# Leaving out three filling products per layer in the router's chain of an encoder kernel

## The reference

```python
g_prob = softmax(xf @ w_group + b_group)            # 4 groups
g_w, g_sel = top_k(g_prob, 1)
e_logits = (xf @ w_router + b_router) of the 8 experts in the picked group
top_v, top_i = top_k(e_logits, 2)
weights = g_w * softmax(top_v)
y = for each token and picked expert e: (silu(x @ w1[e]) * (x @ w3[e])) @ w2[e]
h = h + sum over the two picks of weights * y
```

## Time and profile before

| | before |
|---|---|
| median of three runs | 1776.87 us |
| lowest and highest | 1775.58, 1777.07 us |
| profiled execution, device time | 1775.46 us |
| its span, first to last instruction | 1773.7 us |
| PE busy | 1504.0 us, 85% |
| VectorE busy | 617.1 us, 35% |
| ScalarE busy | 528.3 us, 30% |
| mean granted clock of PE | 0.938 |
| read from HBM | 524.63 MB |

### The profile page before, as it was taken

How to read it: one execution, slowest core, us unless ns; L and a number is a source line. 1 busy time by engine, 2 the same in 40 slices (tenths; PEclk the granted TensorE clock), 3 DMA queues, 4 the chain that set the end, 5 groups by cost and what they waited for, 6 DMA issues and landing times.

```text
span 1773.7 us, 24555 instructions
## 1 busy us (share of the span) xinstructions
PE 1504.0 (85%) x9704; PEld 1009.0 (57%) x9704; DVE 617.1 (35%) x1020; ACT 528.3 (30%) x829; POOL 57.3 (3%) x100
## 2 busy tenths in 40 slices
PE   8999999999886867676799999999998767676766
PEld 7788889896332323232277878998863233333322
DVE  5565777644110000000054668775530101010101
ACT  6434655553200000000163465635431000000001
POOL 3021000000000000000000200000000000000000
PEclk9999999999988888889899999999999988898989
DMA  7545235755999999999955453357469999999997
GB/s 230 190 141 191 102 138 190 274 201 198 405 423 422 422 421 423 422 422 421 416 184 176 125 182 115 136 198 285 150 277 408 422 422 421 422 423 421 422 423 309
DMA packets 118166, 530.92 MB, mean 299 GB/s; under 512 B 8809, under 2 KB 9001, under 8 KB 68935
## 3 DMA queue, kind: packets, MB, share of 16 engines
q1 hardware_dynamic: 114944, 524.13, 74.3%
q0 software_dynamic: 3136, 5.73, 1.6%
q10 hardware_dynamic: 12, 0.05, 0.0%
HBM read 524.63 MB, written 1.05 MB: 296 GB/s over the span
## 4 chain that ended last, share of the span: by engine, by line
PE 55%; DMA 36%; DVE 3%; SPq 2%; ACT 2%; issue 2%; PEldq 0%; POOL 0%; DVEq 0%; ACTq 0%
DMA ring<-in_w_dram 35%; PE ps L2031 11%; PE ps L1667 7%; PE ps L1672 6%; PE ps L1668 6%; PE ps L1701 5%; PE ps L1702 5%; PE ps L1707 5%; SPq L557 2%; PE ps L1749 2%; PE ps L1806 1%; PE ps L2000 1%; PE ps L1829 1%; PE ps L1760 1%; PE ps L1618 1%
## 5 line engine op out<-in xcount | busy, mean ns | idle before, releaser
L2031 PE MATMUL ps<-ring,big 128*32 128x512 f32 x2048 | 299.0, 738 | 205.8 <-DMA ring<-in_w_dram 204.0
L1129 DVE TENSOR_TENSOR weight_split<-ring,weight_split 128x1024 fp32r<-128x1024 f32 x224 | 270.9, 1222 | 168.4 <-ACT weight_split L730 165.7
L2031 PEld LDWEIGHTS ps<-ring,big 128*32 128x32 f32 x2048 | 83.3, 131 | 416.1 <-issue 415.9
L730 ACT ACTIVATE weight_split<-ring 128x1024 fp32r<-128x1024 f32 x224 | 234.3, 1058 | 223.5 <-PE ps L1707 93.0
L1528 DVE TENSOR_TENSOR big<-big,ps 128x256 f32<-128x256 f32 x32 | 13.5, 421 | 696.8 <-ACT big L1018 696.8
L1667 PE MATMUL ps<-operand_split,weight_split 128*128 128x256 f32 x896 | 228.6, 293 | 5.0 <-DVE operand_split L1194 4.4
L1668 PE MATMUL ps<-operand_split,weight_split 128*128 128x256 f32 x896 | 220.5, 283 | 0.0
L1667 PEld LDWEIGHTS ps<-operand_split,weight_split 128*128 128x128 f32 x896 | 171.7, 192 | 18.9 <-issue 17.3
L1014 ACT ACTIVATE big<-ps 128x512 f32<-128x512 f32 x32 | 33.6, 1050 | 474.5 <-PE ps L2031 474.5
L1668 PEld LDWEIGHTS ps<-operand_split,weight_split 128*128 128x128 f32 x896 | 172.1, 192 | 2.0 <-issue 1.9
L1701 PE MATMUL ps<-weight_split,operand_split 128*128 128x512 f32 x384 | 152.8, 398 | 5.2 <-issue 5.2
(11 more groups left out here) (243 smaller groups left out, 1359.8 us busy)
## 6 DMA issues: line engine op xcount, KB each, us to landing
ring<-in_w_dram SPq DMA_DIRECT2D x376, 1024.0 KB, 17.8
ring<-in_w_in_dram SPq DMA_DIRECT2D x28, 2048.0 KB, 8.1
ring<-in_w_xkv_dram SPq DMA_DIRECT2D x8, 2048.0 KB, 8.1
ring<-in_w_attn_out_dram SPq DMA_DIRECT2D x4, 2048.0 KB, 8.3
ring<-in_w_conv_out_dram SPq DMA_DIRECT2D x4, 2048.0 KB, 7.7
ring<-in_w_out_dram SPq DMA_DIRECT2D x4, 2048.0 KB, 8.1
big<-in_w_dram SPq DMA_DIRECT2D x8, 1024.0 KB, 13.7
ring<-in_w_xq_dram SPq DMA_DIRECT2D x4, 2048.0 KB, 8.6
```

The lines of the kernel that those rows point to most:

```text
L730: act.activation(split_quarter(k, 0), landed_quarter(k), ACT.Copy).then_inc(w_hi, 1)
L1129: dve.tensor_tensor(split_quarter(k, 1), landed_quarter(k), split_quarter(k, 0).bitcast(F32), ALU.subtract).then_inc(w_lo, 1)
L2031: last = pe.matmul(ps[CAP * j:CAP * (j + 1), 1, :], xe[:, k, e * CAP:(e + 1) * CAP], pair_slot(j)[:, k, :], start=(k == 0), stop=(k == DC ...
```

## The change

PE no longer issues the three filling products per layer; the helper `again` goes with them. Nothing else changes: the order of the other instructions, the waits, and the other engines are as they were. The banks into which the three wrote are written again by others, before they are read, as before.

```diff
-                def again(count, idle):
-
-                    for _ in range(count):
-                        pe.matmul(ps[:, idle, :], ident, h[:, 1, 0:SLAB], start=True, stop=True)
-
-                again(2, bank("nf3"))
                 pe.wait_ge(*due(r_mask, 1))
                 dst = ps[:, bank("rank"), :]
                 pe.matmul(dst[:, 0:EXPERTS], tri, picked[:, 0, :], start=True, stop=True)
...
-                again(1, bank("router1"))
                 pe.wait_ge(*due(n_ready_act, 4))
                 first_tokens()
                 pair(first=True)
```

## The result

| | before | changed |
|---|---|---|
| median, 22 executions each | 1777.12 us | 1783.97 us |
| lowest and highest | 1773.78, 1782.13 | 1773.75, 1788.22 |
| ratio, 95% interval | | 1.0029 [1.0019, 1.0039] |
| profiled execution, device time | 1775.46 | 1787.15 |
| its span | 1773.7 | 1785.4 |

The change makes the kernel slower, by 0.29% as a ratio and 6.9 us between the medians. The forecast was 1783.5. Single executions spread more than the difference is large, and those of the changed kernel fall into two groups with nothing between: seven from 1773.75 to 1778.54 and fifteen from 1782.26 to 1788.22.

What follows compares the result with a forecast made beforehand. PE's router chain at the expert stage's door was taken to bound the end, the DMA engines waiting there. The profiled 1775.46 us plus 5.5 (layer 0) and 2.6 (layer 1) gave 1783.56, say 1783.5; range 1778.0 to 1785.5.

Steps and rivals of the forecast that it cites:

- The door bounds the end: From the last router products to the first expert pair, DMA waits for PE: a microsecond there is one at the end.
- Layer 0 gets no time back: Layer 0's rank products wait for VectorE's picked experts anyway, so removing the fillings gives back 0 us.
- early fall: Low clock around L1949 and L1974, before the rank products; seen in layer 1, 1298.0 to 1304.7 us; may shift or stay.
- Layer 1 gets 1.5 us back: Layer 1's rank products queue behind the fillings; without them they start 1.72 us earlier, of which 1.5 us is saved.
- The clock falls late: Idle and sparse PE work around the rank products drops the clock to 0.50 at about the gather's start.
- Price of the gather, 3.1 us: The gather's 32 instructions at the low clock take 0.2125 instead of 0.115 us each: 3.1 us, bounds 0 and 3.8.
- Price of the first pair, 2.3 us: The first expert pair's L2031 begins at the low clock and loses 1.7 to 3.35 us, taken as 2.3.
- The sum: Late fall's price at layer 0's door 5.5 us, bounds 1.7 and 7.2; layer 1 adds 2.6 net.
- B: Rival: the clock falls late in one layer only, the other gets its 1.5 us: 1779.5 us, chance 0.26.
- C: Rival: the clock stays high at both doors and PE merely gets out of the way: 1773.9 or 1772.9 us, chance 0.08.
- D: Rival: the clock falls but returns during the gather; a 3.4 us low stretch costs 1.7 once: 1777.2 us, chance 0.07.
- E: Rival: the DMA-bound experts absorb the door's delay: 1775.5 us, or 1774.0 with layer 1's gain, chance 0.05.

Runs made afterwards that it cites:

- e3: Ten filling products instead of two ahead of the rank products, against the kernel before: median 1791.07 us, ratio 1.0080.
- e8: The change itself run once more, all three fillings out in both layers, against the kernel before: median 1783.82 us, ratio 1.0039.
- e10: The three fillings left out in layer 1 only, against the kernel before: median 1778.91 us, ratio 1.0011.
- e7: Residual product moved before the last transposes, half-wide filling before the router's products; of the old fillings only the last kept; against the kernel before: 1790.57 us, ratio 1.0079.
- e6: Residual product moved before the last transposes, half-wide filling before the router's products; none of the three old fillings; against the kernel before: 1787.68 us, ratio 1.0062.
- e2: Only the filling behind the rank products left out, the two ahead kept, against the kernel before: median 1785.76 us, ratio 1.0049.
- e1: The two fillings ahead of the rank products left out, the one behind kept, against the kernel before: median 1777.45 us, ratio 1.0002.
- e11: Residual product and half-wide filling moved into early gaps, fillings ahead of the rank products kept, last one left out; against the kernel before: 1785.26 us, ratio 1.0045.

## Why the prediction held, step by step

- **The door bounds the end.** Right. Shown by e3: two doors 13.0 us longer than in the profile of before, a median 14.1 higher.
- **Layer 0 gets no time back.** Right: with no early fall the rank products wait for VectorE whether PE fills or not. With an early fall, which layer 0 did not have in the profile I worked from, it can get time back as layer 1 does (e8, 22.89 us).
- **Layer 1 gets 1.5 us back.** The mechanism is right where the early fall lasts long: 1.3 us in e10. In the changed kernel's own profile the early stretch of layer 1 lasted 3.2 us instead of 6.7; PE was 0.68 us idle before the picks came, and about 0.9 us was saved. That is an estimate: in e3's layer 1, with an early stretch of the same length, the first filling starts 7.05 us behind L1949's start, two fillings are 1.72, and the rank products of the changed kernel start at 7.90. They start 2.5 us sooner than in layer 1 of before, mostly because the early fall was shorter.
- **The clock falls late.** Right, in both layers of the changed profile, but not at the gather's start: it came some 2 us into the gather (started at 432.22 and 1313.24; low from 434.4 and 1315.0).
- **Price of the gather, 3.1 us.** Right for a whole gather at the low clock (e7: 3.1, e6: 3.3). The late fall of the changed profile came only 2 us into it: +1.5 and +1.9. In e8 it was +2.8.
- **Price of the first pair, 2.3 us.** Measured +1.2 and +2.5 there (8.30 and 9.62 against 7.1), +1.5 in e8, +2.5 and +2.6 in e2 and e7. Here my two prices did not agree with each other: a whole gather at the low clock (6.8 us) and then 2.3 us lost in the pair (4.6 us low) ask for a low stretch of over 11 us, and the longest row I had was 6.7. A stretch of 6.7 us that begins at the gather loses 3.4, not 5.4. The stretches turned out at 6.7 and 10 us in the changed kernel, 10.2 in e8, 13.5 in e6 and 16.8 in e7; that they can be so long no row of before showed me.
- **The sum.** I had 5.5 us for a door without early fall, and e8's layer 1 shows 26.11 - 21.78 = 4.3, the two gathers and pairs of the change 2.7 and 4.4. So the door without early fall was sized too large against e8, and layer 0's in the changed profile, +2.8, is half of it. The two doors together are 5.0 us above before in the changed profile and 2.9 in e8's, and the sum had 8.1. That the median came within 0.5 us of the forecast is in part luck, and has help from the reference: I added 8.1 us to an execution that lay 1.7 below the median of before. Against that median the forecast is +6.4, the measurement +6.9 between medians and 5.2 by ratio (0.29%). How much of that median falls at the doors and how much at later falls of the clock, which shift with them, no run shows.
- **Rivals.** B is real as a part of the mixture: e8's profile is such a door pair, at 1780.32. The executions from 1773.75 to 1778.54 may be the change with one late fall or with none; none of them was profiled, and e8's eleven times show no such gap between two groups. I gave it 0.26; 7 of 22 and, in e8, 1 of 11 lie below 1779.5. C falls for the median: with the fillings out no profile kept the clock up where the early fall was missing too (e8's layer 1, both layers of e6). Where an early fall was long the clock did stay up at the gather, and an execution with two such doors would be C's; that is open. The Trainium skill's warning of long idle gaps ("TensorE: Matmul & The Clock Gate", section "HAM oscillation") does not cover e2, where no gap near the fall is over 0.76 us and the clock falls. D falls: the late low stretches of these profiles lasted 6.7 us and more, not 3.4. E falls by e3.
- **What I did not see.** How far the early and the late fall hang together. A long early fall makes L1974 slow and thereby fills the long gap, and three gathers behind one were spared. e1 against e7 points the same way: the same fillings, 0.5 us against 13.5 us above before, though e7's gap is also 0.86 us longer for the product that was moved. It is no rule: a short early fall spared neither gather of the changed kernel, and in e2 not even the long ones did. I had priced the two falls nearly as if each came by itself.

## What to carry to other kernels

Products that compute nothing can be worth keeping: look at what PE does around each of them, not at whether anyone waits for them. The place counts, and it depends on what stands around it: beside the order of before, the one product between two sparse stretches was worth more than the two in the longer gap (e1 +0.5 us, e2 +8.8); with the forward move it was the other way round (e7 +13.5, e11 +7.7), and only both together were fast. A filling that runs at the low clock costs nearly double (2.06 us against 1.10 in e7). Move real products into the gaps as well, and close the first gap of a chain first, since a fall there can hide what the later ones need; e6 and e7 show that moving alone made it worse. Where executions of one kernel spread by 8 us, a difference of two profiles is not the effect of a change; time many executions and read the profiles for the mechanism alone.

## What the runs showed of the hardware

- The clock can fall while PE has work nearly all the time: in e2 the gather began after 0.76 us idle and ran into the low clock, and in the changed kernel the fall came in the middle of a row of gather products. What such stretches have in common here is small products of 32 to 64 columns with short gaps around them; the same gather in the expert loop, with full products close by, stayed at 1.00.
- Small float32 products take nearly double the time at 1.2 GHz, the same for 36 and for 64 columns: 0.2125 us apart in the earlier trace rows, and 6.93 us for 32 in e7 (0.21 each), where at full clock it is 0.115.
- A kernel on one core, the same program and data, took 1772.55 to 1781.23 us in 29 executions of before on one chip. Part of that can be where the clock fell: L1949 and L1974 took 3.40 and 5.58 us in e1's layer 0, and 2.02 and 3.68 in layer 0 of before, with the same instructions ahead of them.
